# Seven quarter products: sums and low parts made by VectorE alone, each behind the product that frees its slot

## What is computed

```python
def swiglu(h, w_gu, w_down):                     # 1024 -> 2 x 2816 -> 1024
    gate, up = jnp.split(h @ w_gu, 2, axis=-1)
    return (jax.nn.silu(gate) * up) @ w_down
h = h + 0.5 * gate1 * swiglu(modulate(rms_norm(h, n1), shift, scale), w_gu, w_down)
```

## Time and profile before

| | us |
|---|---|
| median of 3 runs | 3559.84 |
| profiled execution | 3560.62 |
| its span, first to last instruction | 3558.8 |
| busy: PE / VectorE / ACT / GpSimd | 3174.7 / 2436.3 / 1409.1 / 1526.6 |
| share of the span | 89% / 68% / 40% / 43% |
| mean granted TensorE clock | 0.955 |

### The profile page before, as it was taken

How to read it: one execution, slowest core, us unless ns; L and a number is a source line. 1 busy time by engine, 2 the same in 40 slices (tenths; PEclk the granted TensorE clock), 3 DMA queues, 4 the chain that set the end, 5 groups by cost and what they waited for, 6 DMA issues and landing times. The chain is left out here.

```text
span 3558.8 us, 66836 instructions
## 1 busy us (share of the span) xinstructions
PE 3174.7 (89%) x27026; PEld 2800.9 (79%) x27026; DVE 2436.3 (68%) x3739; ACT 1409.1 (40%) x2643; POOL 1526.6 (43%) x1028
## 2 busy tenths in 40 slices
PE   4899999899989887999997899999999888788887
PEld 3798899786667776888996898899895677677776
DVE  5777866665676548787767777767665776567665
ACT  3333334224664334233334333334226543434333
POOL 4454445201615226445446454445005162465554
PEclk7999999999999998999998999999999999899999
DMA  3222312342000011223221223311330000122222
GB/s 158 95 89 101 101 66 72 119 150 83 2 17 4 15 53 60 95 99 103 80 69 37 102 78 111 101 61 65 132 139 34 17 3 15 59 74 87 72 78 83
DMA packets 71834, 264.74 MB, mean 74 GB/s; under 512 B 7936, under 2 KB 9088, under 8 KB 70912
## 3 DMA queue, kind: packets, MB, share of 16 engines
q1 hardware_dynamic: 71120, 256.95, 20.8%
q10 hardware_dynamic: 432, 3.88, 0.3%
HBM read 258.70 MB, written 2.10 MB: 73 GB/s over the span
## 5 line engine op out<-in xcount | busy, mean ns | idle before, releaser
L1260 PE MATMUL ps<-m_hi,pair_hi 128*128 128x386 f32 (+1 forms) x1408 | 481.7, 342 | 145.9 <-POOL slot_lo L715 101.7
L1260 PE MATMUL ps<-m_lo,pair_hi 128*128 128x386 f32 (+1 forms) x1408 | 472.5, 336 | 0.0
L1260 PEld LDWEIGHTS ps<-m_hi,pair_hi 128*128 128x128 f32 x1408 | 279.0, 198 | 167.9 <-POOL slot_lo L715 115.0
L877 ACT ACTIVATE pair_hi<-slot_sum 128x512 fp32r<-128x512 f32 x352 | 220.8, 627 | 428.2 <-POOL slot_sum L706 427.4
L1260 PE MATMUL ps<-m_hi,slot_lo 128*128 128x386 f32 (+1 forms) x1056 | 353.8, 335 | 0.0
L735 POOL TENSOR_TENSOR slot_lo<-raw,pair_hi 128x512 fp32r<-128x512 f32 x64 | 90.0, 1419 | 503.3 <-ACT pair_hi L897 262.4
L1113 DVE SCALAR_TENSOR_TENSOR h<-ps,mod,h 128x512 f32<-128x512 f32 x336 | 196.8, 630 | 153.2 <-PE ps L1284 152.6
L911 ACT ACTIVATE tanh_s<-gate_s 128x256 f32<-128x256 f32 (+2 forms) x242 | 116.2, 506 | 430.8 <-DVE gate_s L1067 430.8
L1260 PEld LDWEIGHTS ps<-m_lo,pair_hi 128*128 128x128 f32 x1408 | 279.6, 199 | 0.0
L1260 PE MATMUL ps<-m_hi,w_hi 128*128 128x386 f32 (+1 forms) x704 | 234.9, 334 | 37.2 <-DVE m_lo L1046 25.1
L1284 PE MATMUL ps<-ring_hi,pair_hi 128*128 128x512 f32 (+1 forms) x812 | 230.3, 354 | 15.3 <-DVE slot_lo L735 8.9
(11 more groups left out here) (370 smaller groups left out, 9123.4 us busy)
## 6 DMA issues: line engine op xcount, KB each, us to landing
raw<-wgu SPq DMA_DIRECT2D x176, 512.0 KB, 3.3
w_mod_one<-wmod SPq DMA_DIRECT2D x100, 512.0 KB, 3.4
raw<-wdn SPq DMA_DIRECT2D x88, 512.0 KB, 3.3
raw<-win SPq DMA_DIRECT2D x44, 512.0 KB, 4.6
w_mod_two<-wmod SPq DMA_DIRECT2D x28, 512.0 KB, 3.6
w_mod_first<-wmod_first SPq DMA_DIRECT2D x4, 2048.0 KB, 23.3
raw<-wout SPq DMA_DIRECT2D x16, 512.0 KB, 3.3
h<-xT ACTq DMA_DIRECT2D x1, 3072.0 KB, 8.3
```

Of the source, the lines that this page charges most:

```text
L877: act.activation(flat(slot_hi[p]), quarter(3) if p == 6 else slot_sum[p][:, :], ACT.Copy).then_inc(slot_hi_ready.sem, 1)
L1260: mm = pe.matmul(bank(n, p), w[:, k, :], m[:, k, 0:HW], start=(k == 0 and w is slot_hi[p] and m is M_OF[p][0]), stop=(k == LP - 1 and w is ...
```

## The change

All 716 instructions that GpSimd had in the feed-forward blocks are VectorE's: sums, low parts, normalisations. The second semaphores for GpSimd's results go. In a pair's program each sum stands behind the combine of the product that frees its slot, and silu of both halves is done before the first `glu_out`. ACT makes the gate's high part ahead of the tanh, and slot 6 before slot 5. SP frees a raw buffer on the three sums that read it, not on all four. Down tile 7 uses slot 2 instead of slot 4, so in a down phase of 8 tiles the next pair's sums come in the order 4, 3, 5, 2, and sum 3 is then computed as raw quarter 3 less sum 4, the same value. Modulation products are divided anew: pairs 1, 2, 3 of group 0 and pair 1 of group 2, and five in each down phase of groups 0, 2, 3, 4. GpSimd keeps the squares of the residuals at the end of a block.

```diff
-                    def next_pair(n, first):                     # in GpSimd's program
-                        for p in (2, 3, 5) if first else (2, 3, 4, 5):
-                            weight_sum(pool, p, n)
-                        slot_lo_made(pool, 3, n)
-                        slot_lo_made(pool, 6, n)
...
+                    NEXT_4 = {4: ((weight_sum, 4), (weight_sum, 3)), 5: ((weight_sum, 5), (slot_lo_made, 4), (slot_lo_made, 3)),
+                              6: ((slot_lo_made, 6), (slot_lo_made, 5)), 7: ((slot_lo_made, 2),)}
...
                             if not last_of(n):
                                 gate_lo_made(n + 1)
+                                weight_sum(dve, 2, n + 1)
...
                             with_sixth(n)
                             with_fifth(n)
                             if not last_of(n):
+                                weight_sum(dve, 3, n + 1)
                                 slot_lo_made(dve, 2, n + 1)
...
                             with_seventh(n)
+                            if not last_of(n):
+                                weight_sum(dve, 4, n + 1)
...
                             gate_second(n)
+                            if not last_of(n):
+                                weight_sum(dve, 5, n + 1)
+                                slot_lo_made(dve, 3, n + 1)
+                                slot_lo_made(dve, 4, n + 1)
...
                             up_first(n)
+                            if not last_of(n):
+                                slot_lo_made(dve, 6, n + 1)
                             silu(n, 0)
+                            silu(n, 1)
                             glu_out(n, 0)
-                            silu(n, 1)
                             glu_out(n, 1)
```

More of the change, by code:

```diff
@@ L616, in ffn @@
             counted(hi_at, *((p, 0) for p in (2, 4, 5, 3, 6)))
[L617 to L618 removed]
+            counted(lo_at, *((p, 0) for p in (2, 4, 5, 3, 6)))
             for n in range(N):
@@ L650, in ffn @@
                 count = 0
-                for j in (0, 2, 3):
-                    for key in range(FIRST[j] + (j == 0), FIRST[j] + 4):
-                        mods_of[key] = [count]
+                for j, in_pairs in ((0, (1, 2, 3)), (2, (1,)), (3, ()), (4, ())):
+                    for q in in_pairs:
+                        mods_of[FIRST[j] + q] = [count]
                         count += 1
-                    mods_of["down", j] = list(range(count, 8 * (count // 8 + 1)))
-                    count += len(mods_of["down", j])
+                    mods_of["down", j] = list(range(count, count + 5))
+                    count += 5
             MODS = 24 if mod_plan else 0
@@ L823, in _ @@
-                    pool.wait_ge(hn_hi_ready.sem, hn_hi_ready.at(KD + 1))
-                    for half in range(2):
-                        pool.wait_ge(rstd_ready.sem, rstd_ready.at(half + 1))
-                        pool.tensor_tensor(x_norm[:, half, LP:KD, 0:HT], gained_h[:, LP:KD, half * HT:(half + 1) * HT],
-                                           rstd_of(half), ALU.mult).then_inc(x_pool.sem, 1)
-                        moving_lo((1, 5)[half], lambda k: x_norm[:, half, LP + k.start:LP + k.stop, 0:HW], (5, 11)[half])
@@ L1157, in _, with normed_half @@
[L1157 to L1161 removed]
+                    def normed_half(half, k0):
+                        dve.tensor_tensor(x_norm[:, half, k0:k0 + LP, 0:HT], gained_h[:, k0:k0 + LP, half * HT:(half + 1) * HT],
+                                          rstd_s[:, half * HT:(half + 1) * HT].rearrange("p (a t) -> p a t", a=1)
+                                          .broadcast_to([P, LP, HT]), ALU.mult).then_inc(x_own.sem, 1)
@@ new lines, in moving_sum, with two_lo @@
+                    def moving_sum(out, a, b, op, *after):
+                        for x in after:
+                            dve.wait_ge(x_own.sem, x_own.at(OWN[x]))
+                        for k in two:
+                            dve.tensor_tensor(out[:, k, 0:HW], a(k), b(k), op).then_inc(x_own.sem, 1)
+                    def two_lo(p, x, n_hi):
+                        for i, k in enumerate(two):
+                            moving_lo(p, x(k), k, n_hi + i)
+                    b11, b12 = (lambda k, half=half: x_norm[:, half, k, 0:HW] for half in range(2))
@@ new lines, in _ @@
+                    b21, b22 = (lambda k, half=half: x_norm[:, half, LP + k.start:LP + k.stop, 0:HW] for half in range(2))
+                    t1, t2, t4 = (lambda k, p=p: m_raw[p][:, k, 0:HW] for p in (2, 3, 6))
+                    t3 = lambda k: x_less[:, k, 0:HW]
+                    normed_half(0, LP)
+                    dve.wait_ge(x_own.sem, x_own.at(OWN["X21"]))
+                    two_lo(1, b21, 5)
+                    dve.wait_ge(rstd_ready.sem, rstd_ready.at(2))
+                    normed_half(1, 0)
```

208 lines of the change are left out of this document (86 added, 122 removed).

## The result

The changed kernel takes 3434.81 us (median of 4 runs, 3428.44 to 3436.54). The kernel before took 3558.82 on the same chip; the ratio is 0.9641, 95% interval 0.9615 to 0.9666. So it is 124 us faster where 202 were forecast, and 77 us above the forecast of 3358; it lies 10 us above the range as well. The profiled execution (3428.44 us, span 3426.7, mean granted clock 0.961) is the fastest of the four, 6 us under the median. So a difference between its trace and another's can be some us off the difference of the medians.

A forecast was written before the change was run, and what follows sets the result against it. Feed-forward blocks lose 324 us to PE idle (219) and slow clock (105), PE's longest wait being for GpSimd's low parts. Starts save 67, rests 135, together 202: from 3560.6 to 3358 us, range 3330 to 3400 (3310 to 3425 with rivals).

The forecast's parts named there:

- GpSimd stretched VectorE: Feed-forward blocks: both engines serialize reading two SBUF operands; VectorE's low part takes 1.69 us, 0.68 when GpSimd rests.
- rival 1: VectorE pays full durations, not its pitch, in the denser list: 14.6 us a 768-token pair, 12.8 at 512; 3409 us; 8%.
- Rates of the pairs: VectorE per pair: 13.3 us against PE's 14.8 at 768 tokens; 11.6 against 10.5 at 512, run-ahead covering it.
- The start of a block: VectorE alone makes all operands at block starts: first block passes ring_lo at 145.3, not 162.7; starts save 67 us.
- The ring: Last pair to second ring_lo: 4.3 us against 6.3 of PE work, so the wait goes except in the first group.
- Landings of the raw buffers: Sum 2 waits for a landing low 6 releases; cost taken as 0, since 5.4 us of work covers 3.3.
- In the down phase ... VectorE ... about 31 ... It fits just.: Down phase: VectorE's additions, five modulation products and slot instructions total about 31 us, against PE's 33.6 a group.
- The clock: Rest of each full-width block: 8 us left as lost, for the clock at 0.99 and an odd stall.
- The last tile ... that goes: Last down tile: low part and weights move earlier, so PE's 4.44 us wait for it in a first block goes.
- rival 2: Ring stalls of 3 us a group and slow clock stay; only slot waits and a third of clock loss go: 3424; 17%.
- Rival 3: Slower: if raw-buffer landing took 10 us, it becomes VectorE's period, 17.8 us a 768-token pair; 3612 us; 5%.
- rival 4: All hides: no stall in the rests of the blocks and clock at full, 22 + 16 us more saved: 3320; 8%.

The follow-up runs named there:

- Experiment 8: Changed kernel with slot 6's low parts given back to GpSimd, for all pairs of a block but the first (84 instructions): 3439.64 us.
- Experiment 1: Changed kernel with the down phases' modulation rows not loaded again, VectorE doing the same products on the row already there: 3371.02 us.
- experiment 5: Changed kernel with the same 24 modulation products spread: three instead of five in down phases of groups 2, 3, 4, the rest in pairs: 3393.06 us.
- experiment 9: Changed kernel with the modulation products placed where the kernel before had them: 3400.63 us.
- experiment 2: Changed kernel without GpSimd's squares of residuals 1 to 6 at the end of the feed-forward blocks: 3415.84 us.
- experiment 4: Kernel before the change, without the same GpSimd squares of residuals: 3539.79 us.
- experiment 10: Changed kernel with ACT making down tile 7's high part after the high parts of normalised tiles 0 and 1, not ahead of them: 3422.68 us.
- experiment 3: Changed kernel with both no reloads of modulation rows in the down phases and no squares 1 to 6: 3346.65 us.

## Why the prediction was right or wrong

Right in direction and in what GpSimd had cost VectorE, wrong in size: 124 us came of 202. In the windows 143 us came, and outside them the kernel lost 11, by the traces. By its steps:

- *GpSimd stretched VectorE.* Held. VectorE's low parts last 0.69 with a maximum of 0.695, and its busy time rose by 71 us, where the text said 250 and the plain sum of durations was 490. The collisions had cost more than I gave them. Experiment 8 shows them alone.
- *VectorE pays its pitch and not full durations.* Held, and rival 1 is out: in the dense list behind the first group two low parts of 0.68 us start 0.60 apart (175.45 and 176.05). The rule that I quoted against it from the Trainium skill, "VectorE: DVE Perf Modes", section "The DRAIN you can't avoid", was quoted short: the section adds that an operation which is not held starts earlier, and the rows agree with that.
- *Rates of the pairs.* Held. In the 512-token block the same product starts 11.79 us apart where 11.6 was worked out and 13.6 was measured before. VectorE sets the pace there, and PE waits 0.7 us for it in such pairs, so its run-ahead did not cover as much as I had said. Timeline of PE:

```profile
3065.29 0.39 PE L1247 MATMUL ps<-m_hi,pair_hi 128*128 128x258 f32 x1 [0.71 <-DVE pair_lo L713]
...
3077.08 0.39 PE L1247 MATMUL ps<-m_hi,pair_hi 128*128 128x258 f32 x1 [0.72 <-DVE pair_lo L713]
```

- *The start of a block.* Held for the first block: 90.0 us against 88.7.
- *The ring.* Held in the wide blocks: three stops of 2.1 to 2.2 us are left there, one in each first group, as expected. The 512-token block keeps one in each of its six groups (five of 2.1 to 2.3 and one of 0.55), where only the first was expected; 18.2 us in all, where the text said under 15.
- *Landings of the raw buffers.* Held, at next to nothing. The row of the waits:

```profile
DVE slot_sum L705 <- DMA raw<-wgu: 12.2, 5, 3.4
```

  GpSimd had 205.2 us of them in 69 waits. The slower rival, in which a landing becomes VectorE's period, was wrong for the raw buffers. Its mechanism is the one that struck, but at the modulation rows' buffer, which I had not looked at.
- *"In the down phase ... VectorE ... about 31 ... It fits just."* This step failed. It summed the instructions (the terms given make 30) against PE's 33.6 a group, and put at nothing that each product waits for a load that only the product before it releases. A landing of 3.3 us behind each makes a product every 5.7 us where PE makes a tile in 4.2. The waits are 7 us a down phase: 37 us against 33.6, and the 3.4 us over are the mean of PE's twelve stops. Experiment 1 takes that wait away and leaves the work, and 64 us go; experiment 5 gets 42 of them by placing products where other work covers the landing. The wait had a row before the change too (57.3 us in 30 waits); the change made it 85.9 in 48 by its new division, and experiment 9 prices that at 34 us.
- *The clock.* The prediction left 8 us in each wide rest, with the clock at 0.99. It is 0.99 in the first, and 0.97 in the second and third block. Twelve times 1.6 us at half clock is 19 us by my estimate, near the 20.4 of busy time that experiment 1 gives back. With the 41 us of the stops that is 60 us, about what is missing in the windows (202 less 143).
- *"The last tile ... that goes"* and *"nothing outside them changes".* Failed too. The stop at the last tile went, and its time came back as a wait of the mixer's first product, 15.8 us twice where it was 10.7 in all, for the chain addition, high part, low part at 5.3 us a tile. I read the wait of 4.44 us as a cost without following who ends the block. Two things make this wait. The squares' share was there before: experiment 2 gets 19 us, experiment 4 as much (22) in the kernel before. ACT's early high part of tile 7 is new with the change and belongs to the step that was to end the stop at the last tile; it delays the chain's first high part, and experiment 10 gets 9 to 12 us back by moving it.
- *The rivals.* The time, 3434.8, is nearest to rival 2's 3424, but not by its mechanism: it had the ring's stalls stay, and they fell from 49.8 to 18.2 us. Rival 3's was the period of a landing, for the wrong buffer. In rival 4 nothing was left, and 113 us of idle are. No rival had the modulation rows or the end of a block.

3435 less 64 and 19 is 3352, and both at once gave 3347: the forecast's 3358 is about the time of a kernel without these two losses. Some 46 us of the miss of 77 the change made itself (34 by experiment 9, 12 by experiment 10), if the two add up, which no run shows. The rest would then be losses that the kernel before had too and that the forecast did not see; how it splits is open.

## What to carry to other kernels

When work is added to an engine, sum its instructions and then, separately, work out the period of every single buffer that it reads: use plus issue plus landing. If that period is over what the next engine needs per step, and no other work fills the landing, the work does not fit though its sum does; place such steps where other work fills the landing, or give them a second buffer (not tried here). Before a stop is counted as a gain, follow the chain that ends the stage: a stop ahead of another wait can be worth nothing. And when an instruction is moved ahead on an engine that works in order, ask what now stands behind its wait.

## What the runs showed of the hardware

- Beside GpSimd's squares (1.47 and 2.13 to 2.19 us) VectorE's `hn_lo` takes 3.08 us for two instructions that take 1.15 without them: it starts at 605.71 and ends at 608.79, 0.28 after GpSimd's second instruction (606.33 and 2.18). The Trainium skill, "SBUF — State Buffer", section "Who interferes with whom", makes the shared ports an exclusive lock, held by whoever starts first. The trace agrees that the two serialize, also in the 0.86 us of silu in experiment 8 from 0.52; which of the two held the ports at a given time it does not show.
- I had not expected this to be so complete: 84 low parts given back to GpSimd lightened VectorE by nothing (busy 2521.0 us from 2507.3), and 716 taken from GpSimd cost VectorE 71 us.
- Where PE stops less, its matmuls are mostly shorter too: the same 27026 are busy 3174.7 us before, 3137.4 after and 3115.5 in experiment 3, with the mean granted clock at 0.955, 0.961 and 0.971. It is no fixed rate: in experiment 2 PE's idle time is 20 us less than in the changed kernel and its busy time 8 us more (3145.3).
